# The modulation product of a transformer kernel, from one group of array columns to four 32-column groups

## The reference

```python
for i in range(DEPTH_2):                       # 4 layers
    sh, sc, gt = jnp.split(jax.nn.silu(c) @ ada_w[i] + ada_b[i], 3, axis=-1)
    shc, scc, gtc = jnp.split(jax.nn.silu(c_ctx) @ ada_w[i] + ada_b[i], 3, axis=-1)
    h = rms_norm(x, norm_g[i]) * (1.0 + sc[:, None]) + sh[:, None]
    ...
    x = x + gt[:, None] * ((o * jax.nn.silu(z)) @ w_out)
```

## Time and profile before

| what | value |
|---|---|
| median of 3 runs | 2571.68 us (2567.77 to 2584.24) |
| the profiled execution: its span, first to last instruction | 2584.9 us |
| what the profile shows around that span | nothing further; the execution's own time is not given apart |
| PE busy | 2324.4 us, 90% |
| DVE, ACT, POOL busy | 58%, 39%, 33% |
| mean granted TensorE clock | 0.946 of full |
| matmul records of the modulation product (L435) | 1536, for 768 matmuls |

### The profile page before, as it was taken

How to read it: one execution, slowest core, us unless ns; L and a number is a source line. 1 busy time by engine, 2 the same in 40 slices (tenths; PEclk the granted TensorE clock), 3 DMA queues, 4 the chain that set the end, 5 groups by cost and what they waited for, 6 DMA issues and landing times.

```text
span 2584.9 us, 39576 instructions
## 1 busy us (share of the span) xinstructions
PE 2324.4 (90%) x14736; PEld 1939.2 (75%) x14736; DVE 1492.0 (58%) x2854; ACT 1010.7 (39%) x1843; POOL 845.5 (33%) x544
## 2 busy tenths in 40 slices
PE   6969888999798889899999998999999888879898
PEld 5968788989687888777777785777778555667677
DVE  4594479645944787346663215556323788842565
ACT  3434356443343554443332324332234433224332
POOL 2445333124453331043332123342313433232443
PEclk8989889999898999989999999999999899989998
DMA  6433544554334445431113322112332111123111
GB/s 210 139 97 108 156 147 155 180 155 145 92 112 157 146 144 178 130 121 33 33 35 115 113 90 62 61 58 57 99 98 84 55 41 33 50 90 114 58 58 58
DMA packets 72848, 262.92 MB, mean 102 GB/s; under 512 B 8032, under 2 KB 10208, under 8 KB 72416
## 3 DMA queue, kind: packets, MB, share of 16 engines
q1 hardware_dynamic: 71392, 256.31, 31.4%
q0 software_dynamic: 1280, 4.20, 0.5%
HBM read 259.43 MB, written 1.05 MB: 101 GB/s over the span
## 4 chain that ended last, share of the span: by engine, by line
PE 63%; DVE 24%; issue 5%; ACT 4%; POOL 2%; DMA 2%; ACTq 0%; DVEq 0%; SPq 0%; POOLq 0%
PE gemm L397 12%; PE gemm L399 10%; PE gemm L398 10%; PE gemm L645 6%; PE gemm L435 5%; PE score L684 5%; DVE r L1239 3%; PE obank L716 3%; PE tbank L614 3%; DVE w_lo L292 3%; DVE d L1329 2%; DVE d L1185 2%; PE stat L625 1%; PE obank L720 1%; DMA ring<-wall 1%
## 5 line engine op out<-in xcount | busy, mean ns | idle before, releaser
L292 POOL TENSOR_TENSOR w_lo<-ring,w_hi 128x1024 fp32r<-128x1024 f32 x208 | 508.7, 2449 | 629.8 <-ACT w_hi L829 628.8
L397 PE MATMUL gemm<-g_hi,w_hi 128*128 128x256 f32 x1344 | 404.7, 301 | 72.6 <-DVE w_lo L292 40.5
L829 ACT ACTIVATE w_hi<-ring 128x1024 fp32r<-128x1024 f32 x344 | 362.4, 1054 | 105.9 <-PE gemm L399 34.9
L397 PE MATMUL gemm<-h_hi,w_hi 128*128 128x512 f32 (+1 forms) x928 | 387.4, 417 | 13.8 <-DVE h_lo L1551 8.4
L398 PE MATMUL gemm<-g_lo,w_hi 128*128 128x256 f32 x1344 | 393.4, 293 | 0.0
L399 PE MATMUL gemm<-g_hi,w_lo 128*128 128x256 f32 x1344 | 392.6, 292 | 0.0
L398 PE MATMUL gemm<-h_lo,w_hi 128*128 128x512 f32 (+1 forms) x928 | 352.5, 380 | 0.0
L399 PE MATMUL gemm<-h_hi,w_lo 128*128 128x512 f32 (+1 forms) x928 | 352.2, 380 | 0.0
L397 PEld LDWEIGHTS gemm<-g_hi,w_hi 128*128 128x128 f32 x1344 | 274.6, 204 | 91.5 <-DVE w_lo L292 44.8
L1096 ACT ACTIVATE pr<-score,small 128x512 f32<-128x512 f32 (+1 forms) x192 | 128.1, 669 | 464.9 <-DVE small L1448 464.9
L397 PEld LDWEIGHTS gemm<-h_hi,w_hi 128*128 128x128 f32 x928 | 179.6, 194 | 149.7 <-issue 110.6
(11 more groups left out here) (266 smaller groups left out, 4016.4 us busy)
## 6 DMA issues: line engine op xcount, KB each, us to landing
ring<-wall SPq DMA_DIRECT2D x478, 512.0 KB, 3.7
r<-nbias POOLq DMA_DIRECT2D x16, 256.0 KB, 3.0
cst<-consts SPq DMA_DIRECT2D x1, 2340.5 KB, 10.3
r<-x_t SPq DMA_DIRECT2D x1, 1024.0 KB, 4.9
x<-ctx_t SPq DMA_DIRECT2D x1, 1024.0 KB, 15.5
y_t<-x SPq DMA_DIRECT2D x4, 256.0 KB, 2.3
d<-pos SPq DMA_DIRECT2D x1, 128.0 KB, 10.2
```

The costliest lines, as they stand in the source:

```text
L292: eng.tensor_tensor(w_lo[:, q % SPLITS, :, :], ring[:, t % RING, :, :], w_hi[:, q % SPLITS, :, :].bitcast(F), ALU.subtract)\
L397: pe.matmul(out, w[0][:, k, :], x[0], start=start, stop=False)
L829: act.activation(w_hi[:, q % SPLITS, :, :], ring[:, t % RING, :, :], ACT.Copy).then_inc(S["hi_ready"], 1)
```

## The change

The four matmuls that lie next to each other now write to four different groups of 32 partitions of the PSUM bank (0, 32, 64 and 96), which are four groups of 32 columns of the array, each to columns 0 to 127 of the bank. Before, all wrote to partitions 0 and 1, and to four stretches of columns. For this a weight tile no longer holds 8 chunks of the sum by 128 columns, but 2 chunks by 512 columns, so that each of the four tiles of a row adds to all four stretches. The number of matmuls, their shapes, the number of tiles and of bytes are what they were. ACT now takes a row in four copies of 2 x 128, one from each group of partitions, in place of one of 2 x 512.

```diff
             def ada_row():
                 out = bank()
-                for j in range(4):
+                for i in range(4):
                     w = tile()
-                    for k in range(KC):
-                        ins = pe.matmul(out[0:2, j * P:(j + 1) * P], c_vec[:, k, :], w[:, k, :],
-                                        start=(k == 0), stop=(k == KC - 1))
-                        if k < KC - 1:
-                            yield
+                    for kk in range(2):
+                        k = 2 * i + kk
+                        for j in range(4):
+                            a = 32 * j
+                            ins = pe.matmul(out[a:a + 2, 0:P], c_vec[:, k, :], w[:, 4 * kk + j, :],
+                                            start=(k == 0), stop=(k == KC - 1))
+                            if (kk, j) != (1, 3):
+                                yield
                     tile_done(ins)
                     yield
...
             def ada_row_out():
                 b = op(4)
-                seq(act.activation(ada_rows[0:2, n["row"] % 2, :], b[0:2, :], ACT.Copy))
+                for j in range(4):
+                    ins = act.activation(ada_rows[0:2, n["row"] % 2, j * P:(j + 1) * P], b[32 * j:32 * j + 2, 0:P], ACT.Copy)
+                    if j < 3:
+                        ins.then_inc(S["act_step"], 1)
+                        n["step"] += 1
+                seq(ins)
...
 def pack_weights(a):
-    ada = [a["ada_w_2"][L][:, m * P:(m + 1) * P] for L in range(DEPTH2) for m in range(24)]
+    ada = [a["ada_w_2"][L][2 * i * P:2 * (i + 1) * P, r * 4 * P:(r + 1) * 4 * P] for L in range(DEPTH2) for r in range(6) for i in range(4)]
...
-            tiles.append(w_tile(ada.pop(0)))
+            tiles.append(ada.pop(0).reshape(2, P, 4 * P).transpose(1, 0, 2).reshape(P, KC * P))
```

## The result

| | before | after |
|---|---|---|
| median us (20 executions each) | 2577.55 | 2563.91 (2550.18 to 2578.44) |
| ratio, 95% interval | | 0.9945 [0.9929, 0.9961] |
| profiled execution: span us | 2584.9 | 2564.9 |
| its mean granted clock | 0.946 | 0.925 |

The account below looks back on a forecast made before the run. PE, busy 90% of the span with 63% of the last chain, was the main bound, DVE in the third slot. Layer norms 19.8, starts -5, slots 14.7 gave 29.5 us: 2571.7 to 2542 us, own range 2530 to 2556.

Parts of the forecast that it names:

- A row: Modulation product: a row falls from 7.09 to 3.7 us, a matmul's second record following its first on the same columns.
- Rival A: Modulation rows: all four column groups work at once, a row in 1.9 us; 38 us gained, 2534 us; chance 0.18.
- ACT's copies: ACT taking each row: four copies take 1.1 us, 0.5 us more a row, range 0.1 to 1.7.
- ACT is covered in the slots: Slots: ACT is busy 10 of 34 us, so its copies cost nothing; otherwise six rows would cost 3 us.
- Layer norms: Ten rows in five layer norms: 4.1 us gained in two, 2.9 in two, 5.8 in the last; together 19.8 us.
- rival D: Layer norms: PE's stop before the transposes drops the clock, the variance sums double, 18 us back; 2560 us; chance 0.12.
- the forecast's own signs of being wrong: Modulation rows and layer norms: records not lying beside each other, or PE's stops pulling the clock down inside layer norms.
- Starts of block2: Eight rows: PE waits for POOL, 1.3 us gained, 2.5 lost if the clock falls; 5 us lost, ends -5 and +5.
- Transfers cost nothing: Weight tiles: count and bytes unchanged, layer norm tiles land in time, block2 waits lie inside POOL's time; no cost.
- Slots: Six rows in three slots: PE 6.7 us shorter each, limited by DVE; gains 6.7, 6.0 and 2, together 14.7 us.
- PE comes to 27.3, above 25.0, so 6.7: First slot: PE's shortened time stays above DVE's 25.0 us, taken at the third slot's 0.83 share, so 6.7 us gained.
- What can be told from no change: Whole kernel: about 1%, 26 us, separates a change from none; below 2546 us counts as faster, chance 0.47.

Follow-up runs that it names:

- experiment 6: Changed kernel plus 9 idle float32 matmuls behind the first row of each layer norm: 0.9897 of the kernel before.
- experiment 9: Kernel before with the new rows at the starts of block2 only, plus idle matmuls there: 0.9998 of the kernel before.
- experiment 3: Kernel before with the new rows only in the eight rows at the starts of block2: 1.0039 of the kernel before.
- experiment 4: Kernel before with the new rows only in the six rows of the slots: 1.0007 of the kernel before.
- experiment 1: Kernel before with its old matmuls and tiles, but ACT takes each row in four copies of 2 x 128: 1.0024 of the kernel before.
- 7: Changed kernel plus idle matmuls at layer norms, starts of block2 and slots: 0.9854 of the kernel before; repeated word for word, 0.9860.
- 8: Kernel before with the new rows in the layer norms only, plus 9 idle matmuls behind each first row: 0.9920 of the kernel before.
- experiment 11: Kernel before with seven eighths of one place's row sums left out: slots 1.0006, starts of block2 1.0018, layer norms 0.9928 of the kernel before.

## Why the prediction was half right

- **A row: 3.7 us forecast, 1.93 measured.** Rival A had the mechanism and the price (1.9). The reason for 3.7, that a matmul's two records queue on their columns, didn't show. Alone, this error would have made the kernel faster than forecast: A's sum was 38 us.
- **ACT's copies: 1.1 us forecast, 1.13 measured.** That ACT is covered in the slots was wrong in the first two: its copy stands in the chain at their end, one before and four now, 0.5 us more each.
- **Layer norms: 19.8 us forecast, 21.6 [13, 30] measured.** The sum held by two errors against each other, so that its closeness is partly luck. The distance from the sum for the mean to that for the variance fell from 11.88 to 8.45 us, 3.4 in place of 2.9: the squares' end and then the copies bind, as A said. Against that stands the variance at half clock, 1.7 us or more in four of five. That is rival D's mechanism, and one of the forecast's own signs of being wrong. D put a stop of 1.6 us and a loss of 18 us on it; the stop is 2.67, as the copies wait for the squares, the sums take 9.5 us more, and the whole of what idle work brought back there is 12 (experiment 6).
- **Starts of block2: 5 us lost forecast, 10 [5, 15] lost.** The mechanism was right: POOL is next late, PE stands, the clock falls, the V product begins at half clock. PE stands 2.67 and 2.71 us there in two stops, where the forecast had "some 4" (its own rows give 1105.77 - 1100.4 = 5.3). Idle work removes the loss (experiment 9). "Transfers cost nothing" holds there as well: the rows' waits for tiles lie inside POOL's time. The profile of experiment 3 shows 7 us more in the V products and 9 less in the four stretches before them, where profiles with the old rows differ from one another by up to 3 us a layer; where the 10 us lie is open.
- **Slots: 14.7 us gained forecast, nothing measured.** This is the step that failed. I took "PE comes to 27.3, above 25.0, so 6.7" as if PE's other work kept its duration, and DVE's bound from the share of busy time of another slot. The runs show two things in its place. DVE's own chain is late next earlier than its share of busy time said: with the clock nearly whole the three slots give 3.9, 2.8 and 0 us. And the fillers had kept the clock up: with less to do, PE stands some 2 us for DVE in the middle of the slot, drops to half clock and becomes the bound again with the work that was never changed (117.6 us for the three slots of experiment 4, 117.7 before). With three quarters of the filler matmuls' time gone or with seven eighths of the matmuls gone, the result is the same zero. I had priced the fall of the clock at the starts and named it for the layer norms, and not asked for it here, where PE was busiest.
- **What can be told from no change.** The forecast took 1%, 26 us. The interval of the result is 0.16% to each side, 4 us, so the 14 us are clear of noise.

## What to carry to other kernels

A small-result float32 product packs well into four column groups: about a quarter of the time here (1.93 of 7.09 us), whatever the order within a tile. But filler work on TensorE that shares its place with a chain of another engine is worth what that chain leaves, and it may be what keeps the clock up. Before shortening such filler, take most of it out as an experiment: it is cheap, and told here at once that shortening alone brings nothing in the slots. It says nothing of what is there with the clock kept up; for that, put idle work in the filler's place. Where the filler is gone, a few idle matmuls in the stop in front of dependent TensorE work bring back more than they cost (0.9945 to 0.986 here, the fastest version); where they last longer than the stop, they only delay (1.0062).

## What the runs showed of the hardware

- Four float32 matmuls of 128 columns into four groups of 32 partitions overlap nearly fully, with their two records each: 30 ns from record to record, against 111 in one group; a row is 7.09 / 1.93 = 3.7 times as fast. The Trainium skill (TensorE: Matmul & The Clock Gate, Part 3: Packing small matmuls) has three groups at 2.38 times; the trace of this case is above that, close to the number of groups.
- ACT's copy of 2 x 128 takes 0.27 us from the four partition groups, and four of them 1.13; four from partitions 0 and 1 took 0.74 in experiment 1.
- In the second to fifth layer norm of the changed kernel PE stops 2.67 us between the first row and its transposes. In three of them the clock was at half in the sum behind the stop (0.52 in 300 to 303), in the fifth not. With idle matmuls in the stop (0.46 us left of it in the second) all five sums ran at full clock, in each of the profiles of 6, 7 and 8.
- In the first two slots PE had no stop of over 0.4 us before, and the clock stayed whole. With the new rows PE stands 2.05 and 2.27 us for DVE in them, and the clock fell to half at or behind each (the same in experiment 4, at 2.06 and 2.26). With idle matmuls, at stops of 0.86 and 1.78 us, it held. The length of the stop doesn't settle it alone: in the second slot of experiment 11 the clock fell behind one of 1.51 us.
